# Expert rows fetched and summed by indirect transfers, and expert weights in transfers of four row chunks

## The reference

```python
def moe(x, w_router, wg, wu, wd):
    logits = jnp.einsum('bld,de->ble', x.astype(jnp.float32), w_router.astype(jnp.float32))
    vals, idx = lax.top_k(logits, TOP_K)
    wts = jax.nn.softmax(vals, axis=-1)
    gates = jnp.sum(jax.nn.one_hot(idx, N_EXPERTS, dtype=jnp.float32) * wts[..., None], axis=-2)
    y = jnp.zeros(x.shape, jnp.float32)
    for e in range(N_EXPERTS):
        y = y + gates[..., e:e + 1] * swiglu(x, wg[e], wu[e], wd[e]).astype(jnp.float32)
    return y.astype(x.dtype)
```

## Time and profile before

| | us |
|---|---|
| median of 3 runs | 977.94 |
| lowest and highest run | 977.25, 977.95 |
| profiled execution, whole time | 977.73 |
| its span, first to last instruction | 975.9 |
| PE busy in the span | 926.8 |
| DVE busy | 722.3 |
| ACT busy | 524.6 |
| POOL busy | 122.1 |
| expert part, first gather to last scatter | 505.6 to 934 |

### The profile page before, as it was taken

How to read it: one execution, slowest core, us unless ns; L and a number is a source line. 1 busy time by engine, 2 the same in 40 slices (tenths; PEclk the granted TensorE clock), 3 DMA queues, 4 the chain that set the end, 5 groups by cost and what they waited for, 6 DMA issues and landing times.

```text
span 975.9 us, 14777 instructions
## 1 busy us (share of the span) xinstructions
PE 926.8 (95%) x6085; PEld 809.1 (83%) x6085; DVE 722.3 (74%) x877; ACT 524.6 (54%) x579; POOL 122.1 (13%) x158
## 2 busy tenths in 40 slices
PE   4999989999999997999989999999999999999976
PEld 3999789999999997998867777777777777777775
DVE  3786475655555676885569888898898979898965
ACT  5322354443445354322438877777668667777642
POOL 3337121100110013424210000000000000000001
PEclk9999899999999998998989999999999999999978
DMA  9973355746674657524317986999789988989601
GB/s 320 310 222 104 77 173 167 192 139 216 186 184 137 207 173 194 169 95 110 126 60 264 402 333 244 395 367 345 285 318 357 338 322 319 364 341 380 233 3 45
DMA packets 119798, 224.85 MB, mean 230 GB/s; under 512 B 4882, under 2 KB 88978, under 8 KB 119584
## 3 DMA queue, kind: packets, MB, share of 16 engines
q1 hardware_dynamic: 117664, 216.63, 63.2%
q0 software_dynamic: 2064, 7.23, 3.1%
HBM read 220.31 MB, written 3.99 MB: 230 GB/s over the span
## 4 chain that ended last, share of the span: by engine, by line
PE 82%; DVE 9%; ACT 5%; issue 2%; DMA 1%; POOL 1%; SPq 0%; DVEq 0%; ACTq 0%; POOLq 0%
PE bank L683 13%; PE bank L684 12%; PE bank L685 12%; PE bank L961 7%; PE bank L959 7%; PE bank L960 7%; DVE wlo L1364 5%; PE bank L981 4%; PE bank L983 4%; PE bank L982 4%; ACT whi L1131 2%; PE bank L903 1%; PE bank L904 1%; PE bank L934 1%; PE bank L849 1%
## 5 line engine op out<-in xcount | busy, mean ns | idle before, releaser
L1364 DVE TENSOR_TENSOR wlo<-raw,whi 128x1408 fp32r<-128x1408 f32 (+2 forms) x294 | 480.2, 1653 | 120.4 <-ACT whi L1131 119.9
L1131 ACT ACTIVATE whi<-raw 128x1408 fp32r<-128x1408 f32 (+2 forms) x294 | 398.7, 1381 | 188.2 <-PE bank L685 101.9
L683 PE MATMUL bank<-xh,whi 128*128 128x264 f32 x672 | 197.1, 293 | 19.9 <-DVE xl L1375 11.0
L684 PE MATMUL bank<-xl,whi 128*128 128x264 f32 x672 | 193.7, 288 | 0.0
L685 PE MATMUL bank<-xh,wlo 128*128 128x264 f32 x672 | 193.4, 288 | 0.0
L683 PEld LDWEIGHTS bank<-xh,whi 128*128 128x128 f32 x672 | 130.0, 193 | 21.8 <-DVE wlo L1364 20.3
L959 PE MATMUL bank<-whi,xeh 128*96 128x512 f32 (+1 forms) x384 | 143.7, 374 | 0.6 <-DVE hid L1652 0.6
L961 PE MATMUL bank<-whi,xel 128*96 128x512 f32 (+1 forms) x384 | 143.9, 375 | 0.0
L960 PE MATMUL bank<-wlo,xeh 128*96 128x512 f32 (+1 forms) x384 | 143.5, 374 | 0.0
L684 PEld LDWEIGHTS bank<-xl,whi 128*128 128x128 f32 x672 | 130.2, 194 | 0.4
L685 PEld LDWEIGHTS bank<-xh,wlo 128*128 128x128 f32 x672 | 129.3, 192 | 0.0
(11 more groups left out here) (231 smaller groups left out, 1347.3 us busy)
## 6 DMA issues: line engine op xcount, KB each, us to landing
raw<-in_moe_w_gate SPq DMA_DIRECT2D x32, 1408.0 KB, 6.8
raw<-in_moe_w_up SPq DMA_DIRECT2D x32, 1408.0 KB, 7.6
raw<-in_moe_w_down SPq DMA_DIRECT2D x40, 1024.0 KB, 6.3
raw<-in_w_in SPq DMA_DIRECT2D x20, 1024.0 KB, 7.5
raw<-in_ffn_w_down SPq DMA_DIRECT2D x16, 704.0 KB, 4.9
raw<-in_ffn_w_gate SPq DMA_DIRECT2D x10, 1024.0 KB, 5.4
raw<-in_ffn_w_up SPq DMA_DIRECT2D x10, 1024.0 KB, 5.5
raw<-in_w_o SPq DMA_DIRECT2D x8, 1024.0 KB, 6.5
```

The source lines that it names most:

```text
L683: pe.matmul(out, w_hi, x_hi, start=start, stop=False)
L684: pe.matmul(out, w_hi, x_lo, start=False, stop=False)
L1131: act.activation(unit_hi(u), unit_raw(u), ACT.Copy).then_inc(hi_ready, 1)
L1364: dve.tensor_tensor(unit_lo(u), unit_raw(u), unit_hi(u).bitcast(F32), ALU.subtract).then_inc(lo_ready, 1)
```

## The change

- **Transfers.** Gate, up and down weights of the experts come in transfers of four units (`TURN`), the last of each down matrix in one of three. Gate and up take turns of four units instead of two. The split of the first three banks' gate results (silu) starts after unit 12 of a gu phase instead of 14.
- **Fetching.** After pair 0 is gathered, POOL adds `xth` and `xtl` into `xt` and writes the token rows to a buffer `tokens` in the chip's memory. For pairs 1 to 3 POOL fetches the 96 rows of each expert with an indirect transfer into `xg0`, `xg1`; PE turns them with transposes (`gathered_columns`), four for each block, in the places where the gather blocks stood. `slot_values` of those pairs moves from the end of the d phase ahead, to gu1, gu3 and gu5 after unit 10.
- **Adding.** For experts 0 to 5 ACT writes the scaled output as plain float32 into `ys0` or `ys1`, and POOL adds its 96 rows to a buffer `summed` in the chip's memory with an indirect, adding transfer. Rows of empty slots go to spare rows. `yl`, `pickT`, the scatters and the additions to `h` of these experts are gone. After the sixth addition POOL reads `summed` back into `xt`, and during gu7, from unit 7 on, PE turns it chunk by chunk (`summed_columns`, three transposes each) and DVE adds the eight chunks to `h`. Experts 6 and 7 are scattered as before.

```diff
+TURN = 4
...
-                for _ in range(DC):
-                    add_load(FE, FE)
+                for _ in range(GU_UNITS // TURN):
+                    add_load(*[FE] * TURN)
             else:
-                for _f in range(0, EC, 2):
-                    add_load(*[D] * min(2, EC - _f))
+                for _f in range(0, EC, TURN):
+                    add_load(*[D] * min(TURN, EC - _f))
...
+BY_DMA = NE - 2
+SPARE = T + CAP
...
+RG_AFTER = 10
 FIRST_HID_AFTER = {2: 0, 3: 1, 4: 2}
-SCATTER_AFTER = 1
+SCATTER_AFTER = 7
...
+        xg = [place(f"xg{a}", [P, D], F32, arena + 4 * a * D) for a in range(2)]
+        xt = place("xt", [P, 3, D], F32, arena + 4 * 3 * D)
...
+        ys = [place(f"ys{a}", [P, D], F32, dead + 4 * a * D) for a in range(2)]
...
-                        for k in range(0, DC, 2):
+                        for k in range(0, DC, TURN):
                             for i, src in enumerate((gate, up)):
-                                load(u + 2 * k + 2 * i, src[k * P:(k + 2) * P, :], 2, FE)
+                                load(u + 2 * k + TURN * i, src[k * P:(k + TURN) * P, :], TURN, FE)
                     else:
-                        for f in range(0, EC, 2):
-                            n = min(2, EC - f)
+                        for f in range(0, EC, TURN):
+                            n = min(TURN, EC - f)
...
+            def gathered_columns(p, g, b):
+
+                a, half = divmod(g, 2)
+                if half == 0:
+                    pe.wait_ge(xg_in[a], 16 * p)
+                for c in range(4):
+                    mm = pe.transpose(b[:, c * CAP:(c + 1) * CAP], xg[a][0:CAP, (4 * half + c) * P:(4 * half + c + 1) * P],
+                                      ident[0:CAP, 0:CAP])
+                mm.then_inc(ga_full, 1)
+
+            def summed_columns(m):
+
+                b = bank[6 + m % 2]
+                if m == 0:
+                    pe.wait_ge(sum_in, 48)
+                if m < 2:
+                    pe.wait_ge(y_hi, 2 * BY_DMA)
+                else:
+                    pe.wait_ge(h_added, m - 1)
+                for j, w in BLK:
+                    mm = pe.transpose(b[:, j * P:j * P + w], xt[0:w, j, m * P:(m + 1) * P], ident[0:w, 0:w])
+                mm.then_inc(sc_full, 1)
...
-                k, up = i // 4 * 2 + i % 2, i // 2 % 2
+                k, up = i // (2 * TURN) * TURN + i % TURN, i // TURN % 2
                 p = e // 2
                 pe.wait_ge(lo_ready, u + 1)
-                if e % 2 == 0 and i % 4 == 0:
-                    pe.wait_ge(xe_lo, STEPS_IN * p + k // 2 + 1)
+                if e == 0 and not up and k % 2 == 0:
+                    pe.wait_ge(xe_lo, k // 2 + 1)
+                elif e % 2 == 0 and i % 8 == 0:
+                    pe.wait_ge(xe_lo, STEPS_IN * p + k // 4 + 1)
...
                 if i == 0 and e == 0:
                     pe.wait_ge(hl_ready, 3)
+                elif i == 0 and e <= BY_DMA - 1:
+                    pe.wait_ge(y_hi, 2 * e)
+                    pe.wait_ge(rg_ready, min((e + 3) // 2, PAIRS))
                 elif i == 0 and e < NE - 1:
-                    pe.wait_ge(h_added, DC * e)
+                    pe.wait_ge(h_added, DC)
...
-                            if e >= 2 and 0 <= i - SCATTER_AFTER < DC:
-                                scatter(e - 2, i - SCATTER_AFTER)
+                            if e % 2 and e < NE - 1 and i == RG_AFTER:
+                                if e > 1:
+                                    pe.wait_ge(y_hi, 2 * (e - 1))
+                                else:
+                                    pe.wait_ge(hl_ready, 3)
+                                pe.wait_ge(pick_ready, (e + 1) // 2 + 1)
+                                slot_values((e + 1) // 2, bank[6])
+                            if e == BY_DMA + 1 and 0 <= i - SCATTER_AFTER < DC:
+                                summed_columns(i - SCATTER_AFTER)
...
                                 p, g = e // 2 + 1, GATHER_AFTER[i]
-                                if g == 0:
-                                    pe.wait_ge(pick_ready, p + 1)
                                 if g < 3:
                                     pe.wait_ge(hid_ready, 3 * (e + 1) + g + 1)
                                 else:
                                     pe.wait_ge(xe_lo, STEPS_IN * p + 1)
-                                gather(p, g, bank[3 + g % 3])
-                                if g == 3:
-                                    pe.wait_ge(xe_lo, STEPS_IN * p + 2)
-                                    slot_values(p, bank[4])
+                                gathered_columns(p, g, bank[3 + g % 3])
                             if e == NE - 1 and i in LAST_SCATTER_AFTER:
...
-                act.wait_ge(unit_used, U_FF[1] + MOE_AT["gu", e] + GU_UNITS - 2)
+                act.wait_ge(unit_used, U_FF[1] + MOE_AT["gu", e] + GU_UNITS - TURN)
...
+                if 2 <= e <= BY_DMA:
+                    act.wait_ge(sum_added, 16 * (BY_DMA if e == BY_DMA else e - 1))
+                dst = ys[e % 2] if e < BY_DMA else yh
                 for half in range(2):
-                    act.activation(yh[0:CAP, half * 512:(half + 1) * 512], bank[y_bank(e) + half][0:CAP, :], ACT.Copy,
+                    act.activation(dst[0:CAP, half * 512:(half + 1) * 512], bank[y_bank(e) + half][0:CAP, :], ACT.Copy,
                                    scale=rgs[0:CAP, e // 2 % 2, e % 2, 1 + e:2 + e]).then_inc(y_hi, 1)
...
+                dve.wait_ge(rg_ready, p + 1)
                 if p + 1 < PAIRS:
                     picks(p + 1)
+                token = rgs[0:CAP, p % 2, :, VALS - 1]
+                if p >= 2:
+                    dve.wait_ge(sum_added, 16 * (2 * p - 2))
+                if p:
+                    dve.tensor_scalar(from_row[0:CAP, p % 2, :], token, -1.0, 0.0, ALU.add, ALU.max).then_inc(rows_ready, 1)
+                else:
+                    step(dve.tensor_scalar(spare[0:CAP, :], C("tokid", CAP)[:, 0:1], float(T), None, ALU.add))
+                if p < BY_DMA // 2:
+                    step(dve.scalar_tensor_tensor(out=empty[0:CAP, :], in0=token, scalar=0.0,
+                                                  in1=spare[0:CAP, :].to_broadcast([CAP, 2]), op0=ALU.is_equal, op1=ALU.mult))
+                    dve.scalar_tensor_tensor(out=to_row[0:CAP, p % 2, :], in0=token, scalar=-1.0, in1=empty[0:CAP, :],
+                                             op0=ALU.add, op1=ALU.add).then_inc(rows_ready, 1)
 
             def hid_lo(e, s, b):
...
             def y_out_lo(e):
 
+                if e < BY_DMA:
+                    return
                 for half in range(2):
...
+            def gather(p):
+
+                for a in range(2):
+                    pool.wait_ge(rows_ready, (1, 3, 5)[p - 1] + 1)
+                    if p == 1:
+                        pool.wait_ge(ga_full, STEPS_IN)
+                    else:
+                        pool.wait_ge(ga_full, STEPS_IN * (p - 1) + 2 * a + 2)
+                    pool.indirect_dma_start(xg[a][0:CAP, :], None, tokens[:, :],
+                                            bass.IndirectOffsetOnAxis(from_row[0:CAP, p % 2, a:a + 1], 0)).then_inc(xg_in[a], 16)
+
+            def add_rows(e):
+
+                pool.wait_ge(rows_ready, (1, 3, 5)[e // 2])
+                pool.wait_ge(y_hi, 2 * e + 2)
+                pool.wait_ge(sum_added if e else sum_clear, 16 * max(e, 1))
+                pool.indirect_dma_start(summed[:, :], bass.IndirectOffsetOnAxis(to_row[0:CAP, e // 2 % 2, e % 2:e % 2 + 1], 0),
+                                        ys[e % 2][0:CAP, :], None, compute_op=ALU.add).then_inc(sum_added, 16)
+
+            def experts():
+
+                pool.wait_ge(ga_full, STEPS_IN)
+                pool.tensor_tensor(xt[:, :, :], xth[:, :, :].bitcast(F32), xtl[:, :, :].bitcast(F32), ALU.add).then_inc(xt_free, 1)
+                pool.wait_ge(xt_free, 1)
+                for j, w in BLK:
+                    pool.dma_start(tokens[j * P:j * P + w, :], xt[0:w, j, :]).then_inc(xt_out, 16)
+                pool.wait_ge(xt_out, 48)
+                for p in range(1, PAIRS):
+                    gather(p)
+                    for e in (2 * p - 2, 2 * p - 1):
+                        add_rows(e)
+                pool.wait_ge(sum_added, 16 * BY_DMA)
+                for j, w in BLK:
+                    pool.dma_start(xt[0:w, j, :], summed[j * P:j * P + w, :]).then_inc(sum_in, 16)
...
+                    pool.dma_start(summed[0:T, :], t["zeros"]).then_inc(sum_clear, 16)
```

More of the change, by code:

```diff
@@ L475, in program @@
         flag = moe("flag", [1, 1], I32)
+        empty = moe("empty", [P, 2])
+        spare = moe("spare", [P, 1])
+        from_row, to_row = moe("from_row", [P, 2, 2], I32), moe("to_row", [P, 2, 2], I32)
         pickT = moe("pickT", [P, T], F32R)
@@ L537, in program @@
         o_used, o_silu, o_done, o_scaled = sem("o_used"), sem("o_silu"), sem("o_done"), sem("o_scaled")
```

(25 more changed lines are left out.)

30 lines of the change are left out of this document (15 added, 15 removed).

## The result

| | before | after |
|---|---|---|
| median of 4 runs, us | 977.6 | 1004.4 |
| lowest and highest, us | 976.5, 978.0 | 1002.2, 1005.3 |
| profiled execution, its span, us | 977.7, 975.9 | 1002.2, 1000.2 |
| after / before, 95% interval | | 1.027 [1.025, 1.029] |

The account below looks back on a forecast made before the run. The prediction took PE to bound the expert part, with transfers close behind. From 977.7 us it took 22.1 for PE, added 5.0 for the start and 2.7 for the sum: 963.3, or 963.5 on the median's scale, range 956 to 981.

Parts of the forecast that it names:

- PE's saving: Expert part: removed gather and scatter matmuls save 28.1 us, new transposes cost 6.0, leaving 22.1 us.
- The ring in the middle: Loads issued eight units ahead have first unit ready at t + 11.9, PE wants it at t + 15.3: no cost.
- the prediction's own term: Transfer time of a 2.88 MB load of four units with the engines full at 421 GB/s: 6.85 us.
- The start: Refilling the ring in gu0, with waits at units 8 and 12 and token-row writes, costs 5.0 us (4.3 to 6.9).
- The wait at unit 8: In gu0 PE reaches unit 8 at 528.8, its load is ready at 531.9: 3.1 us of wait.
- PE's second wait: Units 12 to 15 of gu0 are ready at 540.7, PE reaches them at 539.5: 1.2 us of wait.
- POOL's addition is covered: Addition for `xt` takes POOL 5.7 us, DVE can lose about 5; PE's wait covers it, otherwise up to 2 us.
- The fetch without a wait: Rows fetched in gu1, gu3, gu5 are wanted after 12 us, taken as landing 5.8 plus 2 issue: no wait.
- The sum: Adding and reading back take 18 us after d5, PE arrives after 15.3: a wait of 2.7 us (0 to 10).
- Transfers become the bound: Rival: each fetch and addition holds expert weights up 5.8 us, 30 us for six experts: 993.5 us; slower, chance 0.20.
- the four numbers: Times of the forecast and three rivals: 963.5, partly eaten 971.5, transfers the bound 993.5, does not pay 977.5 us.
- Partly eaten: Rival: late middle loads, late sum or clock falls eat some gain: 971.5 us, range 967 to 976, chance 0.20.

Follow-up runs that it names:

- j: f without POOL's addition for `xt`, writes, fetches, adding transfers and reads of the sum; PE, ACT and DVE do all their work: 954.9 us.
- b: The kernel before with transfers and gate/up turns of four units and the earlier silu, gather and scatter still by matmul, POOL idle: 995.2 us.
- a: The changed kernel with transfers of two units (`TURN` = 2), all indirect fetching and adding kept: 969.9 us.
- f: The changed kernel with transfers of two units and the transposes of the sum moved from gu7 into d6: 961.9 us.
- r: m with the order of four gate and four up units and the earlier silu, in transfers of two units: 963.6 us.
- d: The changed kernel with the transposes of the sum in d6 after units 2 to 9, in banks 3 and 4, instead of in gu7: 999.3 us.
- n: The changed kernel with ring places and moment of issue unchanged, each transfer of four issued as two of two units with their own landing: 983.6 us.
- c: The changed kernel with the slot values of pairs 1 to 3 four units earlier, after unit 6 instead of 10 of gu1, gu3, gu5: 999.4 us.
- o: The changed kernel with DVE waiting, after it has made a pair's row numbers, until POOL has issued both fetches of it: 1000.9 us.
- s: m with DVE waiting after a pair's row numbers until POOL has issued both fetches: 960.4 us.
- t: r with DVE waiting after a pair's row numbers until POOL has issued both fetches: 958.7 us.
- m: f with POOL making `xt` in three additions of 128 x 1024, after units 13, 17 and 21, each third's rows written at once: 959.4 us.
- k: f with POOL's addition for `xt` only after unit 1 of gu1 is used: 960.7 us.

## Why the prediction was wrong, step by step

- **PE's saving, 22.1 us: right.** j measured 22.0, give or take 1.5. That sum and its rows stand.
- **The ring in the middle, 0 us with a margin of 3.4: wrong, and the largest miss: 32 us, what it adds at the start included.** Two numbers failed. The margin was measured to the moment when PE wants a unit (t + 15.3). But ACT and DVE run four units ahead of PE, and that lead is what hides every small lateness; ACT wants the unit at t + 7.6. And the landing of t + 8.9 is that of a transfer alone in the queue (three such loads took 9.6 to 10.8). A load behind another has first to wait for it, up to 6.85 us more by the prediction's own term, so up to 15.7; the page has 13.4 for gate. All of these are over 7.6, so ACT had to wait. The row to read was not PE's, which never waited, but ACT's. Its wait of 0.5 us for transfers said only that there was some reserve, not how much. Loads of half the size already landed in 7.2 us at the median, nearly the whole of the 7.6 us that the change left.
- **The start, 5.0 us: the place was right, the terms were not.** The wait at unit 8 came, 5.0 us instead of 3.1, at 532, because the load, alone in the queue, landed 10.8 us after its issue instead of 8.9. The next load landed after 13.0 us, and after 9.6 in b, where no token rows are written: 3.4 us more, where the sum had 0.7 for the writes. PE's second wait was nevertheless 0.5 us instead of 1.2. That POOL's addition is covered by the first wait came true, but only just, and for transfers of four: it took 7.94 us and not 5.7, DVE was at the load's first unit at 530.9, and b, without the addition, has the same wait of 5.0 us. With transfers of two, where no such load is due, the cover is gone and PE waited 4.0 us at the same place. The clock was left out of the sum though the prediction had a row for it: the stage has 0.85, before 0.91. That row says less than was read from it: PE had not been near idle since 500.9, it was busy for 0.79 us of 503 to 504.
- **The fetch without a wait: wrong with transfers of four** (11.8 us of PE), right with transfers of two (a: none, f: 1.1), as long as the issue met no long row of splits (r: 7.8). 12 us were allowed and 2 + 5.8 taken; the issue took 8.0, and the landing 9.7 us at the least. The prediction had the cause in hand, since it quoted POOL and DVE slowing each other, and used it for the addition only.
- **The sum, 2.7 us: mechanism right, size wrong.** The wait was 7.4 us, and with the clock behind it 9 us by a against f. Beside transfers of four its removal gained 5 (d). The addition landed about 9 us after issue where 5.8 stood, and the reads took about 10.
- **The rivals.** "Transfers become the bound" was right in its sign, and its 993.5 is the nearest of the four numbers by luck; its reason was not right. It charged POOL's transfers for holding up the weights, and b shows 19.6 us of loss, and 75.5 of ACT's 86 us of waits, without any of them. The engines' capacity was not short: the DMA share of the part is 0.85. The loss is in the size of the single transfer: it lands whole or not at all, and its place is refilled whole. "Partly eaten" (971.5) is what a, the indirect part alone, shows: 969.9, by the late sum and a clock fall, as it said.

The account, in us against before, each from a pair of kernels: -22.0 (j), +7.0 for POOL's work, nearly all at the start (f against j), +9 for the sum (a against f), +13 for the late refill, most of it by the fetch of pair 2 (n against a), +20 for landing four at once (after against n). They make 27, and must, since each kernel is the next one's base; what they say is the price of each step in this order. In the kernel after the terms can't be had one by one: c, d and o each took a wait of 7 to 12 us away and gained 3 to 5.

On size, the Trainium skill speaks for larger transfers: "DMA: Bandwidth & Descriptors", section Bandwidth, rates larger transfers nearer to the peak. Here 421 GB/s were moved from 540 to 550 us with loads of 2.9 MB, and 421 before with 1.4. So the trace shows no gain, where the queue was full, to set against the loss.

## What to carry to other kernels

Measure a transfer's slack to the first engine that touches the data, not to the one that sets the time, and count its landing behind the transfer that is still under way. In a ring that holds only three transfers, halving their size gave back 32 us and cost nothing in rate. A late weight need not show as a wait for weights: here part of the price came as a fetch issued at the wrong moment. When work is taken off the bound engine, price the idle engine's steps beside their neighbours: here POOL's work at the start and the late sum turned a gain of 2.2% (j) into one of 0.6% (a).

## What the runs showed of the hardware

- The issue of an indirect fetch on POOL takes 0.92 to 1.00 us while DVE is held still (o, s, t: 18 issues) and up to 8.03 us while DVE runs splits with two operands in SBUF in a row. The long issues ended 0.8 to 0.9 us after that row in after, d, m, n and r, and 0.3 us before its end in c. Three plain writes took 1.62 us beside such splits (k).
- POOL's addition of 128 x 3072 took 7.84 to 7.98 us; thirds of it took 2.40 to 3.65 us. A DVE step with two operands that started under it was held to its end: 6.32 us for 128 x 3 instead of 0.15.
- A load of 2.9 MB, alone in the queue, landed 9.6 to 10.8 us after its issue (three cases in after); behind others one took 19.5.
- In after, beside a full weight queue, a fetch of 96 rows of 4 KB landed 9.7 us after issue at the least (10.4 at the median), and an addition of as many rows to memory after 8.8 to 9.5 us. With transfers of two the medians of a are 9.6 and 9.0.
- After a PE wait of 7.4 us (a) the granted clock stood at 0.50 for a stage of 5 us of which PE was busy for 3.6, and at 0.99 in the next.
